# Both attentions of an encoder: scores two units ahead, and the values product at another place in TensorE's order

## The reference

```python
def _block_attention(q, k, v, scale):
    ...
        sc = jnp.einsum('bqkgd,bskd->bkgqs', qi, k,
                        preferred_element_type=jnp.float32) * scale
        p = jax.nn.softmax(sc, axis=-1).astype(v.dtype)
        return jnp.einsum('bkgqs,bskd->bqkgd', p, v)

def _mla(h, w_in, g_q, w_uq, g_kv, w_ukv, w_o, pos):
    proj = h @ w_in                       # compressed q, compressed kv, rotary key
    ...
    q = (_rms(c_q, g_q) @ w_uq).reshape(b, s, HA, DN + DR)
    q = jnp.concatenate([q[..., :DN], _rope(q[..., DN:], pos, ROPE_THETA_A)], axis=-1)
    kv = (_rms(c_kv, g_kv) @ w_ukv).reshape(b, s, HA, DN + DV)
    ...
    o = _block_attention(q, k, v, (DN + DR) ** -0.5)
    return o.reshape(b, s, HA * DV) @ w_o

def _gqa_axial(h, w_qkv, g_qn, g_kn, w_o, row, col):
    proj = h @ w_qkv
    ...
    q = _axial_rope(_rms(q, g_qn), row, col)
    k = _axial_rope(_rms(k, g_kn), row, col)
    o = _block_attention(q, k, v, HD ** -0.5)
    return o.reshape(b, s, HB * HD) @ w_o
```

## Time and profile before

| what | us |
|---|---|
| median of 3 runs | 2402.73 (2401.96 to 2403.64) |
| the profiled execution | 2399.06 |
| its span in the trace | 2397.3 |
| PE busy | 2181.4 (91%) |
| DVE busy | 1694.8 (71%) |
| ACT busy | 1298.8 (54%) |
| POOL busy | 719.0 (30%) |
| latent prelude | 0 to 99.5 |
| latent groups | 99.5 to 387.5 |
| grouped prelude | up to 1145.9 |
| grouped groups | 1145.9 to 1611.2 |

### The profile page before, as it was taken

The page is one execution under the profiler, slowest core; times in us unless marked ns, Lnnn a source line. Parts: engine busy times, 40 slices in busy tenths (PEclk is TensorE's granted clock), DMA queues, the critical chain, the costliest instruction groups (busy, mean ns, idle before and its releaser), DMA issues. The chain is left out here.

```text
span 2397.3 us, 31526 instructions
## 1 busy us (share of the span) xinstructions
PE 2181.4 (91%) x10404; PEld 1604.7 (67%) x10404; DVE 1694.8 (71%) x1916; ACT 1298.8 (54%) x1528; POOL 719.0 (30%) x622
## 2 busy tenths in 40 slices
PE   8899997969999999987899999949969999999993
PEld 5566665747777777756677777737856777777772
DVE  3566664578888888873777777744268888888883
ACT  3344443147777777753544444333117777777773
POOL 1233331011332243215444444420001332333222
PEclk9999999979999999998999999979979999999997
DMA  7000003759999999942111111053269999999983
GB/s 266 3 12 12 11 13 129 277 216 379 383 385 391 388 383 383 395 140 88 45 49 49 51 48 48 14 193 103 99 247 345 386 381 387 389 380 383 396 301 127
DMA packets 176091, 519.86 MB, mean 217 GB/s; under 512 B 13120, under 2 KB 56896, under 8 KB 174976
## 3 DMA queue, kind: packets, MB, share of 16 engines
q1 hardware_dynamic: 168832, 493.53, 54.5%
q0 software_dynamic: 7168, 25.17, 4.5%
HBM read 480.91 MB, written 37.75 MB: 216 GB/s over the span
## 5 line engine op out<-in xcount | busy, mean ns | idle before, releaser
L1844 DVE TENSOR_TENSOR m_w_lo<-s_raw,m_w_hi 128x2048 fp32r<-128x2048 f32 x384 | 865.8, 2288 | 143.1 <-ACT m_w_hi L1788 142.0
L1788 ACT ACTIVATE m_w_hi<-s_raw 128x2048 fp32r<-128x2048 f32 x384 | 730.6, 1915 | 175.3 <-PE m_ps_down L1891 77.7
L1759 POOL DMA_INDIRECT acc<-m_ye,m_row_scatter x32 | 47.0, 1470 | 685.1 <-ACT m_ye L1805 685.1
L1889 PE MATMUL m_ps_gate<-m_w_hi,m_xeT_hi 128*96 128x512 f32 x512 | 205.4, 401 | 3.8 <-DVE m_xeT_lo L1850 3.8
L1889 PE MATMUL m_ps_down<-m_w_hi,m_hidT_hi 128*96 128x512 f32 x512 | 202.6, 396 | 3.8 <-DVE m_hidT_lo L1850 3.8
L1889 PE MATMUL m_ps_up<-m_w_hi,m_xeT_hi 128*96 128x512 f32 x512 | 203.7, 398 | 0.0
L1891 PE MATMUL m_ps_gate<-m_w_hi,m_xeT_lo 128*96 128x512 f32 x512 | 203.3, 397 | 0.0
L1891 PE MATMUL m_ps_down<-m_w_hi,m_hidT_lo 128*96 128x512 f32 x512 | 203.0, 397 | 0.0
L1891 PE MATMUL m_ps_up<-m_w_hi,m_xeT_lo 128*96 128x512 f32 x512 | 202.1, 395 | 0.0
L1890 PE MATMUL m_ps_gate<-m_w_lo,m_xeT_hi 128*96 128x512 f32 x512 | 201.9, 394 | 0.0
L1890 PE MATMUL m_ps_down<-m_w_lo,m_hidT_hi 128*96 128x512 f32 x512 | 201.4, 393 | 0.0
(11 more groups left out here) (234 smaller groups left out, 4435.1 us busy)
## 6 DMA issues: line engine op xcount, KB each, us to landing
s_raw<-in_w_gate SPq DMA_DIRECT2D x128, 1024.0 KB, 8.0
s_raw<-in_w_up SPq DMA_DIRECT2D x128, 1024.0 KB, 7.7
s_raw<-in_w_down SPq DMA_DIRECT2D x128, 1024.0 KB, 8.1
s_raw<-in_w_qkv_b SPq DMA_DIRECT2D x16, 512.0 KB, 4.5
s_raw<-in_w_qkv_b SPq DMA_DIRECT2D x32, 256.0 KB, 5.6
s_raw<-in_w_o_b SPq DMA_DIRECT2D x1, 8192.0 KB, 24.4
acc<-o_x SPq DMA_DIRECT2D x12, 512.0 KB, 5.3
xn<-o_xn SPq DMA_DIRECT2D x12, 512.0 KB, 4.1
```

The lines of the kernel that those rows point to most:

```text
L1759: pool.indirect_dma_start(out=io.acc, out_offset=bass.IndirectOffsetOnAxis(ap=row_scatter[:, :], axis=0), in_=ye[:, :], in_offset=None, co ...
L1788: act.activation(hi[:, split, :, :].rearrange("p k n -> p (k n)"), raw[:, slot, :], ACT.Copy).then_inc(hi_ready, 1)
L1844: dve.tensor_tensor(lo[:, split, :, :].rearrange("p k n -> p (k n)"), raw[:, slot, :], hi[:, split, :, :].rearrange("p k n -> p (k n)"), A ...
L1889: pe.matmul(out[:, cols], left_hi[:, k, :], hi[:, split, kk, cols], start=(k == 0), stop=False)
```

## The change

**The scale.** It no longer stands in exp and maximum. `dve_max` is one instruction, a maximum that is negated as it is written; `act_exp` has no scale. Instead the latent attention scales the queries as ACT copies them and the rotary table once (DVE, new, L695 after the change), and the grouped attention scales the queries' gain once (POOL). DVE's new instruction stands between the norms of token tiles 0 and 1 and waits for all four tables:

```diff
@@ Core.dve_max
         dve.wait_ge(self.scores_done, n + 1)
-        wait(dve, self.negmax_done, n)
-        dve.tensor_reduce(self.rowmax[:, unit % 2, :], self.S[:, unit % 2, :, 0:nk * P], AX.X,
-                          ALU.max).then_inc(self.rowmax_done, 1)
-        dve.wait_ge(self.rowmax_done, n + 1)
         wait(dve, self.exp_done, 2 * n - 2)
-        dve.tensor_scalar(self.negmax[:, unit % 2, :], self.rowmax[:, unit % 2, :], -self.scale, None,
-                          ALU.mult).then_inc(self.negmax_done, 1)
+        dve.tensor_reduce(self.negmax[:, unit % 2, :], self.S[:, unit % 2, :, 0:nk * P], AX.X,
+                          ALU.max, negate=True).then_inc(self.negmax_done, 1)
@@ mla_block, vector
             norm.dve_tile(dve, 0)
+            dve.wait_ge(tables_landed, 64)
+            dve.tensor_scalar(rope_T[2 * DR:, :], rope_T[2 * DR:, :], SCALE, None, ALU.mult).then_inc(rope_scaled, 1)
...
                     core.dve_copy(dve, n, unit)
                     if not (last and unit == NU - 1):
                         core.dve_rinv(dve, n + 1, (unit + 1) % NU)
-                    if not last:
-                        piece(g + 1, 1 - slot, unit)
-                    core.dve_out(dve, g, n, unit, first)
                     if not (last and unit >= NU - 2):
                         core.dve_max(dve, n + 2, (unit + 2) % NU)
+                    core.dve_out(dve, g, n, unit, first)
+                    if not last and unit:
+                        piece(g + 1, 1 - slot, unit - 1)
                     split_by_unit(split, g, unit)
@@ mla_block, tensor
                     core.pe_turn(pe, n, unit, shared.ident[:, :])
-                    if not last:
-                        piece(g + 1, unit)
-                    pe.wait_ge(piece_act, g * NU + (2 if unit < 2 else NU))
-                    core.pe_pv(pe, n, unit, lambda t: V[:, slot, t, head * DV:(head + 1) * DV])
                     if unit < NU - 2:
                         scores(g, slot, unit + 2)
                     elif not last:
                         scores(g + 1, 1 - slot, unit + 2 - NU)
+                    pe.wait_ge(piece_act, g * NU + (2 if unit < 2 else NU))
+                    core.pe_pv(pe, n, unit, lambda t: V[:, slot, t, head * DV:(head + 1) * DV])
+                    if not last:
+                        piece(g + 1, unit)
@@ gqa_block, gpsimd
             pool.wait_ge(tables_landed, 48)
+            pool.tensor_scalar(gains[:, 0, :], gains[:, 0, :], HD ** -0.5, None, ALU.mult).then_inc(gain_scaled, 1)
+            pool.wait_ge(gain_scaled, 1)
@@ gqa_block, scalar
                     core.act_copy(act, n, unit)
...
+                    if unit == 1:
+                        core.act_exp(act, n + 1, 2)
+                    elif unit and not (last and unit >= NU - 2):
+                        core.act_exp(act, n + 2, (unit + 2) % NU)
                     if not last:
                         projected(g + 1, 1 - slot, unit)
+                    if unit == 0:
+                        turned(g, slot, TILES - 1, core.proj)
+                    elif not last:
                         turned(g + 1, 1 - slot, unit - 1, core.proj)
+                    if unit == 1:
+                        core.act_exp(act, n + 2, 3)
@@ gqa_block, tensor
-                else:
+                elif part != 1:
                     pe.wait_ge(qkT_split, m - 1)
...
-                for k in range(KD):
+                for k in range(KD) if part is None else range(part * HALF_K, (part + 1) * HALF_K):
...
                     core.pe_turn(pe, n, unit, shared.ident[:, :])
+                    if unit == 1:
+                        scores(g, slot, 2)
+                    elif unit:
+                        next_scores(g, slot, unit, last)
                     if not last:
-                        project(g + 1, 1 - slot, unit)
+                        project(g + 1, 1 - slot, unit, 0)
+                    core.pe_pv(pe, n, unit, lambda t: V[:, slot, t, :], lambda t: V_lo[:, 1 - slot, t, :])
+                    if not last:
+                        project(g + 1, 1 - slot, unit, 1)
                     if unit == 0:
                         turn(g, TILES - 1, core.proj)
                     elif not last:
                         turn(g + 1, unit - 1, core.proj)
-                    core.pe_pv(pe, n, unit, lambda t: V[:, slot, t, :], lambda t: V_lo[:, 1 - slot, t, :])
-                    if unit < NU - 2:
-                        scores(g, slot, unit + 2)
-                    elif not last:
-                        scores(g + 1, 1 - slot, unit + 2 - NU)
+                    if unit == 1:
+                        scores(g, slot, 3)
```

More of the change, by code:

```diff
@@ L181, with __init__ @@
 class Core:
[L188 to L189 removed]
+    def __init__(self, s, dk, dv, o_dram, probs, probsT, out, probsT_lo=None):
+        self.dk, self.dv, self.o_dram = dk, dv, o_dram
         self.S = s.psum("scores", [P, 2, 2, SAMPLE])
@@ L567, in piece @@
                 if p == 0:
-                    last = act.activation(qT[0:DN, 2 * slot, 0:PROMPT], bank[0:DN, PROMPT:], ACT.Copy)
+                    last = act.activation(qT[0:DN, 2 * slot, 0:PROMPT], bank[0:DN, PROMPT:], ACT.Copy, scale=SCALE)
                 if p == 1:
-                    act.activation(qT[0:DN, 2 * slot + 1, 0:PROMPT], bank[0:DN, 0:PROMPT], ACT.Copy)
+                    act.activation(qT[0:DN, 2 * slot + 1, 0:PROMPT], bank[0:DN, 0:PROMPT], ACT.Copy, scale=SCALE)
                     last = act.activation(V[:, slot, 0:PROMPT_TILES, :].rearrange("p t n -> p (t n)"),
@@ L573, in piece @@
                 if p in (3, 4):
-                    last = act.activation(qT[0:DN, 2 * slot + p - 3, PROMPT:N], bank[0:DN, :], ACT.Copy)
+                    last = act.activation(qT[0:DN, 2 * slot + p - 3, PROMPT:N], bank[0:DN, :], ACT.Copy, scale=SCALE)
                 if p == 5:
@@ L617, in step @@
                     core.act_copy(act, n, unit)
-                    if not (last and unit == NU - 1):
-                        core.act_exp(act, n + 1, (unit + 1) % NU)
+                    if not (last and unit >= NU - 2):
+                        core.act_exp(act, n + 2, (unit + 2) % NU)
                     if not last:
@@ L1160, in step @@
                     core.dve_copy(dve, n, unit)
+                    if unit == 1:
+                        core.dve_max(dve, n + 1, 2)
+                    elif unit and not (last and unit >= NU - 2):
+                        core.dve_max(dve, n + 2, (unit + 2) % NU)
                     if not (last and unit == NU - 1):
@@ L1166, in step @@
                         rotate(g * NU + NU + unit - 1, unit - 1)
-                    if unit == 0:
-                        turned(g, slot, TILES - 1, core.proj)
+                    core.dve_out(dve, g, n, unit, first)
                     if not last:
@@ L1171, in step @@
                         values_low(g + 1, 1 - slot, unit)
-                        if unit:
-                            turned(g + 1, 1 - slot, unit - 1, core.proj)
-                    core.dve_out(dve, g, n, unit, first)
-                    if not (last and unit >= NU - 2):
-                        core.dve_max(dve, n + 2, (unit + 2) % NU)
+                    if unit == 0:
+                        turned(g, slot, TILES - 1, core.proj)
+                    elif not last:
+                        turned(g + 1, 1 - slot, unit - 1, core.proj)
+                    if unit == 1:
+                        core.dve_max(dve, n + 2, 3)
                     if unit in (2, 4) and not (isinstance(g, int) and g >= GROUPS - 2):
@@ L1197, in project @@
                     last = pe.matmul(out, xnT_lo[:, k, at], w_hi[:, slot, k, :], start=False, stop=(k == KD - 1))
-                last.then_inc(proj_done, 1)
+                if part != 0:
+                    last.then_inc(proj_done, 1)
             def turn_x(t):
@@ L1224, in scores, with next_scores @@
                                         head, 2)
+            def next_scores(g, slot, unit, last):
+                if unit < NU - 2:
+                    scores(g, slot, unit + 2)
+                elif not last:
+                    scores(g + 1, 1 - slot, unit + 2 - NU)
             for i in range(TILES + 2):
```

30 lines of the change are left out of this document (14 added, 16 removed).

## The result

The changed kernel takes 2483.27 us (median; 2482.62 to 2485.57), the kernel before 2402.35 beside it: 1.0338 times as long (95% interval 1.0320 to 1.0356), 81 us more. The forecast was 2455 with a range up to 2480: right in direction, 28 us short, and out of its range by 3. The rival with the lower clock stood at 2475.

The account below looks back on a forecast made before the run. PE was taken as the bound in the latent prelude, latent groups and grouped steps. Terms 47 + 4.4 + 8.9 + 3 - 6 - 5 = +52 on the median 2402.73 gave 2455 us, range 2436 to 2480.

Parts of the forecast that it names:

- The rival with the lower clock: Grouped steps: PE's clock falls behind two waits of 2.7 us a step, +20, 2475 us; chance 0.17.
- The sum: Grouped attention, steps 0 to 5: unit times with PE's waits for DVE add to 67.0 us a step, +47 in six.
- The first rival: Grouped steps: lower clock behind waits in six steps, each of two costing 1.7 us: +20, 2475; chance 0.17.
- the prediction's own sign of being wrong: Gaps ahead of values product under 1 us, 128x512 matmuls over 0.4 us behind them, or compress starting before 20.
- step 6: Grouped attention without weight splits: units 3 and 5 take 10.0, the step 62.0 against 57.62, +4.4 us.
- Latent prelude: DVE waits for and scales the rope table, so PE's compress starts at 24.0 instead of 15.12: +8.9 us.
- Latent groups: Seven groups: only scores stand between turn and values product, 7.7 us idle where 4.9 is now: +3.
- The last group: Last latent group: four of six gaps ahead of values products filled with scores: -6 us (-5 to -6.5).
- End of the grouped attention: Output weights' load issued earlier, last unit's scores leave the end of PE's work: -5 us (-6 to -2).
- the copies in time: Grouped steps: DVE copies before half 0 ends, only waits at half 0 left: 2411; chance 0.13, whole or in part.
- the gain of all idle time: Seven grouped steps: DVE runs a whole stage ahead of PE, all idle goes, -26, total 2378 us; chance 0.03.
- the table's wait hidden: Latent prelude: scaling doesn't hold up tile 1, so 8.9 is missing: 2446 us; chance 0.06.

Follow-up runs that it names:

- the fills: Changed kernel plus ten zero-adding matmuls in units 3 and 5 and eight overwritten ones in units 0 and 1 of grouped steps: 2461.92 us.
- the later scaling: Latent attention as changed, grouped in old order, rotary table scaled behind the third token tile's copy instead of ahead of the second tile's norm: 2398.83 us.

## Why the prediction was wrong

**The step that failed is the clock.** The sum put slow matmuls behind the new waits at nothing. The first rival named the mechanism and priced it at +20; the fills measured 21. That the two agree is partly chance: the rival had twelve waits at 1.7 each and nothing for units 0 and 1; between the profiled executions of the changed kernel and of the one with both fills, units 3 and 5 lost 18.1 by it and units 0 and 1 another 6. I gave it 0.17 and left it out of the forecast on one argument: that the matmuls of 128x256 kept their mean of 0.28 through five steps with 17.7 us of waits. That was no evidence for this case. Those waits were 1 to 1.8 us each, and the mean over five steps tells nothing of the matmuls behind one gap. The row that did bear on it was the 2.75 us idle with 0.41 behind it. My own sum made two waits a step of 2.6 to 2.7, as near to it as could be, and I called them "a little shorter"; they were 2.88 to 2.92, slow matmuls follow 11 of the 12, and with 0.63 for 128x512 behind them the prediction's own sign of being wrong came true. The trace before spoke both ways, though. PE also idled 2.59 us at full clock three times in the last group's values products, and two of these times no slow matmul followed, as here:

```profile
1599.91 0.36 PE L262 MATMUL b_ps_probsT<-b_probsT_hi,b_V 128*128 128x256 f32 x1 [2.59 <-DVE b_probsT_lo L330]
1600.11 0.28 PE L263 MATMUL b_ps_probsT<-b_probsT_lo,b_V 128*128 128x256 f32 x1
```

So a part of the rival's 20 belonged in the sum, and its chance was too low. The page "TensorE: Matmul & The Clock Gate" of the Trainium skill, section "HAM oscillation — how this bites in real kernels", tells of a kernel that starts each stretch of matmuls at the lower clock behind DMA waits of about 3 to 5 us. These are longer than the waits in the grouped steps here, so the page doesn't decide this case; the trace does.

**The lengths were right without the clock, but for one term that was too small.** Unit by unit the sum held to 0.2 us in units 0, 1, 2 and 4, and in step 6 (62.0 forecast, 61.72 measured). In units 3 and 5 the copy ended at T+8.4 instead of T+8.1, because DVE's split took 3.15 in place of the 2.74 of the row that I took, and the values product began 0.15 behind it; with the clock held these units take 13.08 for 12.5, 12 times 0.6, some 7 us. The trace before had both lengths: 2.74 where DVE came to the split without idle time, and this where it had waited for ACT's part, as it always does in the new order:

```profile
1437.15 3.15 DVE L1090 SCALAR_TENSOR_TENSOR s_w_qkv_lo<-s_raw,s_g_attn_b,s_w_qkv_hi 128x512 fp32r<-128x512 f32 x4 [0.35 <-ACT s_w_qkv_hi L1014]
```

Unit 2 has the right length with a wrong wait, 0.98 (0.81 in steps 1 and 6) where I had 2.1:

```profile
1399.61 0.36 PE L260 MATMUL b_ps_probsT<-b_probsT_hi,b_V 128*128 128x256 f32 x1 [0.98 <-DVE b_probsT_lo L324]
```

The scores that unit 1 makes at its end lie behind unit 2's T (1391.89 here), and I left them out of PE's side: it was through with half 0 at T+6.7, not T+5.5. The length is set by the end of the copy, and that was right. Units 0 and 1 were long in some steps by the clock too, behind waits of 2 us that I had not thought enough.

**Latent prelude:** +8.9 forecast, +7.8 at the compress, +6.3 by the first scores; the table was scaled at

```profile
18.58 0.56 DVE L695 TENSOR_SCALAR a_rope_T<-a_rope_T 64x768 f32<-64x768 f32 x1 [9.14 <-DMA a_rope_T<-in_rope_a_T]
```

in 0.56 us, below the 0.69 that I had as the lower end. The Trainium skill's page "VectorE: DVE Perf Modes", section "Mode 2×_2P", by which I had estimated about 0.5, was nearer than the row that I took the time from. The compress of all tiles was 1.1 us shorter than before, and the rest of the difference lies in the pieces.

**Latent groups:** seven groups, idle 7.5 us ahead of the values product (7.7 forecast); up to the end of their last values product they took 3.5 us more (+3 forecast). The last group's waits:

```profile
L258 PE MATMUL a_ps_probsT<-a_probsT_sb,a_V 128*64 128x256 f32 x40 | 9.9, 385 | 1.7 <-DVE a_probsT_sb L321 1.7
```

1.7 instead of 7.4; it took 26.8 us instead of 30.6, so -3.8 where I had -6: two gaps of 0.87 stay in units 4 and 5, which have no scores to put between.

**End of the grouped attention:** the load of the output weights is issued at T (1648.17, T also at 1648.17) instead of 3.3 behind it, and from T to the last values product it takes 45.2 us instead of 48.8: -3.6, within the range of -6 to -2.

**The other rivals:** the copies in time and the gain of all idle time didn't come; nor was the table's wait hidden, as the later scaling shows. The share that stays open: behind waits of about 2 us in units 0 and 1 the clock fell in steps 0, 2 and 3 of the changed kernel, but not in 1, 4, 5 and 6, with the same instructions; and one wait of 2.9 had no slow matmuls behind it. What tells them apart I can't say from these runs.

## What to carry to other kernels

When work is taken out from between a producer and the instruction that waits for it, sum both sides from the same zero point, unit by unit: the time until the last of the producers' queue is through (with all that stands in front of it there), and the work that the waiting engine has left. Where that leaves PE idle for about as long as idle time in the trace behind which matmuls were slow, count slow matmuls into the sum, in the share in which the trace shows them, and not among the risks. A side job such as a weight split belongs where its engine waits anyway; moving those, in both attentions at once, gained 17 us here, more than all that was kept of the change (3 us).

## What the runs showed of the hardware

Ten matmuls of zeros made the kernel faster: with them PE idled 0.58 us instead of 2.88 ahead of the same late copy, and the 128x512 matmuls behind took 0.40 us instead of 0.63. Idle time of PE has two prices here, the wait itself and, in most of units 3 and 5, 1.5 us of slower matmuls behind it; in the unit shown these began 1.1 us after work did. Waits of 0.98 us had no such price in any unit 2, those of about 2 us had it in some steps, those of 2.59 at full clock in the kernel before once in three, those of 2.9 in 11 of 12. Length alone doesn't decide: with the whole projection ahead of the values product, matmuls were slow behind a wait of 1.21 us too (unit 0 of step 5).
